# One hybrid attention and SSD layer on one core: gated attention written over its gate, V's tile in places of its own, decays loaded in halves, scores half a chunk sooner, a new order in each head

## The chip, the cores and the metric

The kernel runs on one core of one Trainium2 chip. The metric is the time of one execution on the device in microseconds (us); below 1% this kernel's runs do not tell a change from none. Engines are named as the profile names them: PE (TensorE, matmuls), PEld (its weight loads), DVE (VectorE), ACT (ScalarE), POOL (GpSimd), SP (SyncE). An engine works through its own list in order; it waits where an instruction needs a semaphore that another engine or a DMA has yet to raise.

## The reference, cut to what matters

```python
h = rmsnorm(x, pre_norm_g);  proj = h @ w_in        # 2048 -> q, k, v, z_attn, z_ssm, xBC, dt
o = dilated_attention(q, k, v, rel_bias_table)      # 16 heads x 128, three windows merged
attn_out = rmsnorm(o, attn_norm_g) * silu(z_attn)
ssm_out = ssd_branch(z_ssm, xBC, dt_raw, ...)       # conv, bidirectional chunked scan, D skip, gate, norm
mix = concat([attn_out, ssm_out]) @ w_out
y = x + rmsnorm(mix, post_norm_g)                   # once for 512 prompt rows, once for 256 sample rows
...
# ssd_scan, one direction, chunks of 128 rows:
decay = exp(a_cs[l] - a_cs[s])                      # within a chunk, causal
y_diag = (C B^T * decay) @ xc                       # "within"
y_off = C @ state_before_chunk * exp(a_cs)          # "across"
```

## The kernel before, in words

The 512 prompt rows and the 256 sample rows are held together as T = 768 columns, features on the partitions. Float32 matrices are multiplied in three passes: each operand is split into a rounded part (`_hi`, made by ACT) and the rest (`_lo`, made by DVE), and PE adds hi*hi, hi*lo and lo*hi. Up to about 1271 us of the span PE makes most of the projections and parks them in DRAM (`zx_scr`: V, both gates `za` and `zs`, the SSD's x, half of Q). The stretch that the change touches follows: sixteen turns of `head(a)`, a = 0 to 15, one attention head and two SSD heads each, written out by hand on every engine. From about 1975 us on comes the output projection, which is not touched.

In each `head(a)` PE also works through the rest of the projection (`stream_half`: 12 half chunks a head, for K and half of Q of the heads to come), as filler between the steps of the head. Its steps: `within_chunks(a - 1)` (y_diag of the head before, reads `decay`), `scores(a)` and `scores_of_sample(a)`, `turn_probs(a)` (transposes of the probabilities), `turn_probs_of_sample(a)`, `attend(a)`, `turn_x(a)`, `turn_v(a + 1)` (transposes of x, and of the next head's V), `across_chunks(a)` (y_off). Head a's scores stand in four banks of `ps`, from which DVE takes them (`biased_maxima`, which writes `probs`), ACT makes the exponentials (`exp_of_scores`), and DVE scales them (`normalised`).

Buffers are few, and that makes the waits. `oT`, the attention output, is the front of `probs`: so `biased_maxima(a)` waits until the store of the gated `oT` of head a - 1 has landed in DRAM (`ua_stored`). `decay` (128 x 3072 numbers: two directions, d = 0 and d = 1, of 1536) is loaded from `loc_scr` by one DMA on ACT's queue, `load_decays`, once `within_chunks(a - 1)` has read its d = 0 part, which holds the weights summed over both directions (`weights_in_chunks`, semaphore `wmat_done`). Then DVE subtracts (`decay_differences`, which stands ahead of `normalised` in its list), limits (`decay_limited`), ACT takes the exponential (`exp_of_decays`) and DVE weights (`weighted_decays`). `vT` holds V of the next head; it is loaded by `load_v_and_x` after `attend`. POOL issues the stores of the gated results and the loads of `er`, `cb` (every fourth head) and Q.

The waits that the prediction uses most:

```python
def scores(a):                      # PE
    pe.wait_ge(tile_out, tile_of("k", a) + 1)
    ...
        pe.wait_ge(diag_read, a)    # y_summed(a - 1) on DVE has read what within_chunks(a - 1) left in ps
def turn_probs(a):
    pe.wait_ge(normed, 6 * a + 4)   # normalised(a) on DVE
```

## Time and profile before

| | |
|---|---|
| time, median of 3 runs | 2471.28 us (2469.89 to 2485.74) |
| profiled execution, own time | 2472.09 us |
| its span in the trace | 2470.3 us |
| granted TensorE clock, mean | 0.993 |
| PE busy | 2409.2 us, 98% |
| DVE busy | 1786.7 us, 72% |
| ACT busy | 995.1 us, 40% |

Busy is time in which an engine had at least one instruction under way; PE's instructions overlap, so a busy PE isn't PE at its peak. The span leaves out 1.8 us around the trace. The three runs' median lies 0.8 us below the profiled execution.

### The profile page before, as it was taken

What the parts mean: (1) busy time and instruction counts of PE and PEld (TensorE: products, weight loads), DVE (VectorE), ACT (ScalarE), POOL (GpSimd) and SP (SyncE); (2) the same over time, 40 slices, a digit from 0 to 9 for tenths busy, and PEclk for the clock granted to TensorE, in tenths of its full rate; (3) what the DMA queues carried; (4) which work ended last, traced back from release to release, by engine and by line L of the source; (5) the groups of instructions that cost most, each with busy time, mean ns of one, the idle gap of its engine ahead of it and who ended that gap; (6) DMA issues with size and microseconds to landing.
All of it is one profiled execution on the core that took longest, in us unless ns stands there. A gap on an engine that the chain in (4) does not pass through costs nothing. (4 is left out here: it accounts for less than half of the span.)

```text
span 2470.3 us, 36360 instructions
## 1 busy us (share of the span) xinstructions
PE 2409.2 (98%) x13604; PEld 2280.5 (92%) x13604; DVE 1786.7 (72%) x2563; ACT 995.1 (40%) x1664; POOL 466.1 (19%) x750
## 2 busy tenths in 40 slices
PE   7999999999999999999999999999999999999998
PEld 7999999999999999999998889899889888888887
DVE  5676766666666677777758778777878768777867
ACT  6333433333333333333335455454545532333332
POOL 0000277777773011111100000000000000000000
PEclk9999999999999999999999999999999999999999
DMA  5235466666665344443474555556555435445544
GB/s 167 72 112 182 126 198 206 204 205 200 200 199 158 114 128 132 127 125 119 122 242 145 184 184 160 182 179 193 156 192 167 139 133 170 151 156 130 175 160 164
DMA packets 318345, 398.81 MB, mean 161 GB/s; under 512 B 22822, under 2 KB 238310, under 8 KB 315287
## 3 DMA queue, kind: packets, MB, share of 16 engines
q1 hardware_dynamic: 266103, 225.20, 29.8%
q0 software_dynamic: 29168, 95.62, 12.2%
q10 hardware_dynamic: 22960, 76.53, 9.0%
q8 instruction: 65, 1.06, 0.2%
q14 instruction: 49, 0.40, 0.0%
HBM read 309.02 MB, written 95.59 MB: 164 GB/s over the span
## 5 line engine op out<-in xcount | busy, mean ns | idle before, releaser
L1166 PE MATMUL ps<-h_hi,w_hi 128*128 128x384 f32 x1088 | 365.2, 336 | 0.0
L1166 PE MATMUL ps<-h_lo,w_hi 128*128 128x384 f32 x1088 | 365.0, 335 | 0.0
L1166 PE MATMUL ps<-h_hi,w_lo 128*128 128x384 f32 x1088 | 364.6, 335 | 0.0
L2443 DVE TENSOR_TENSOR w_lo<-raw_qk,w_hi 128x512 fp32r<-128x512 f32 x272 | 214.3, 789 | 154.6 <-ACT w_hi L1696 153.2
L1166 PE MATMUL ps<-t_hi,w_lo 128*128 128x384 f32 x816 | 276.0, 338 | 0.0
L1166 PE MATMUL ps<-t_hi,w_hi 128*128 128x384 f32 x816 | 275.6, 338 | 0.0
L1166 PE MATMUL ps<-t_lo,w_hi 128*128 128x384 f32 x816 | 275.0, 337 | 0.0
L1696 ACT ACTIVATE w_hi<-raw_qk 128x512 fp32r<-128x512 f32 x272 | 171.2, 630 | 244.7 <-PE ps L1166 244.7
L1030 PE MATMUL ps<-h_hi,w_hi 128*128 128x384 f32 x768 | 205.2, 348 | 0.0
L1166 PEld LDWEIGHTS ps<-h_lo,w_hi 128*128 128x128 f32 x1088 | 204.3, 188 | 0.0
L1166 PEld LDWEIGHTS ps<-h_hi,w_lo 128*128 128x128 f32 x1088 | 204.2, 188 | 0.0
L1166 PEld LDWEIGHTS ps<-h_hi,w_hi 128*128 128x128 f32 x1088 | 204.2, 188 | 0.0
L1030 PE MATMUL ps<-h_lo,w_hi 128*128 128x384 f32 x768 | 197.5, 338 | 0.0
L1030 PE MATMUL ps<-h_hi,w_lo 128*128 128x384 f32 x768 | 197.0, 337 | 0.0
L1166 PEld LDWEIGHTS ps<-t_hi,w_lo 128*128 128x128 f32 x816 | 153.3, 188 | 0.0
L1166 PEld LDWEIGHTS ps<-t_hi,w_hi 128*128 128x128 f32 x816 | 153.1, 188 | 0.0
L1166 PEld LDWEIGHTS ps<-t_lo,w_hi 128*128 128x128 f32 x816 | 153.1, 188 | 0.0
L2443 DVE TENSOR_TENSOR w_lo<-stage,w_hi 128x512 fp32r<-128x512 f32 x136 | 99.9, 735 | 71.5 <-ACT w_hi L1696 71.0
L2752 DVE TENSOR_TENSOR stage<-stage,ps 128x512 f32<-128x512 f32 x144 | 97.1, 685 | 71.8 <-PE ps L1328 70.9
L1696 ACT ACTIVATE w_hi<-stage 128x512 fp32r<-128x512 f32 x136 | 85.6, 630 | 151.1 <-PE ps L1166 114.5
L1399 ACT ACTIVATE w_hi<-w_raw 128x512 fp32r<-128x512 f32 x140 | 85.6, 626 | 150.5 <-PE ps L911 88.4
L1328 PE MATMUL ps<-h_hi 128*128 128x512 f32 x372 | 145.2, 390 | 0.0
(370 smaller groups left out, 5411.9 us busy)
## 6 DMA issues: line engine op xcount, KB each, us to landing
raw_qk<-in_w_in SPq DMA_DIRECT2D x102, 512.0 KB, 4.3
w_raw<-in_w_in SPq DMA_DIRECT2D x144, 256.0 KB, 3.5
stage<-loc_scr ACTq DMA_DIRECT2D x16, 1536.0 KB, 11.9
stage<-t_scr SPq DMA_DIRECT2D x48, 512.0 KB, 3.8
stage<-zx_scr ACTq DMA_DIRECT2D x61, 384.0 KB, 5.2
stage<-in_w_out SPq DMA_DIRECT2D x36, 512.0 KB, 3.7
stage<-in_w_in SPq DMA_DIRECT2D x34, 512.0 KB, 4.2
zx_scr<-w_raw SPq DMA_DIRECT2D x34, 384.0 KB, 3.3
```

The lines of the kernel that those rows point to most:

```text
L1030: last = nc.tensor.matmul(ps[:, 2 * parity + b, 0:HALF_T], w, h[:, k * T + b * HALF_T:k * T + (b + 1) * HALF_T], start=(c == 0 and kk == 0 ...
L1166: ins = nc.tensor.matmul(ps[:, bank, 0:HALF_T], w, h(k), start=(start and kk == 0 and q == 0), stop=(last and kk == KC - 1 and q == 2), sk ...
L1328: last = nc.tensor.matmul(ps[:, bank, :], m, w, skip_group_check=True, start=(k == 0 and q == 0 and (p == 0 or not chained)), stop=(k == G ...
L1399: nc.scalar.activation(w_hi[:, c, :], w_raw[:, c, :], ACT.Copy).then_inc(w_hi_done, 1)
L1696: nc.scalar.activation(w_hi[:, n_slot(n, pp), :], src, ACT.Copy).then_inc(w_hi_done, 1)
L2443: nc.vector.tensor_tensor(w_lo[:, n_slot(n, pp), :], src, w_hi[:, n_slot(n, pp), :].bitcast(f32), ALU.subtract).then_inc(w_lo_done, 1)
L2752: ins = nc.vector.tensor_tensor(acc[:, o:o + NBW], acc[:, o:o + NBW], ps[:, bank, :], ALU.subtract if turned else ALU.add)
```

## The change

- `attention_gated` writes `oT * za` into `za` and not into `oT`, and POOL stores `za`. The wait for `ua_stored` leaves `biased_maxima` on DVE and stands on ACT ahead of the load of the next `za`, which moves from `load_head` to `load_behind_scores`.
- V is loaded into two pieces that lie elsewhere (`v_part`, 384 columns each, in `sq_c` and `loc_ssum`), by two DMAs, right after V of the head before has been copied out of `ps`: about a head sooner.
- `load_decays(a, d)`: d = 1 is loaded near the end of the head before, after `wmat_done`; d = 0 as before after `within_chunks`.
- PE: `scores(a)` starts one half chunk sooner, two half chunks instead of one stand between the two turns of probabilities, one instead of two between `attend` and `turn_v`, three instead of two ahead of `across_chunks`.
- New order in each head on ACT and DVE, and in the preparation of head 0, where POOL holds its loads of `er` and `cb` until V has landed.

```diff
+        v_part = (sq_c[:, P:P + HALF_T], loc_ssum[:, TT * 64:TT * 64 + HALF_T])
...
-                pool.dma_start(u_scr[a * P:(a + 1) * P, :], oT).then_inc(ua_stored, 16)
+                pool.dma_start(u_scr[a * P:(a + 1) * P, :], za).then_inc(ua_stored, 16)
...
             load_q(0)
+            pool.wait_ge(v_in, 32)
             load_er(0)
...
             def turn_v(i):
-                pe.wait_ge(v_in, 16 * i + 16)
+                pe.wait_ge(v_in, 32 * i + 32)
...
-                stream_halves(a, 1, 2)
+                stream_halves(a, 1, 1)
                 scores(a)
                 scores_of_sample(a)
-                stream_halves(a, 3, 4)
+                stream_halves(a, 2, 4)
                 turn_probs(a)
-                stream_halves(a, 7, 1)
+                stream_halves(a, 6, 2)
                 turn_probs_of_sample(a)
                 attend(a)
+                stream_halves(a, 8, 1)
                 turn_x(a)
-                stream_halves(a, 8, 2)
                 if a < LAST:
                     turn_v(a + 1)
-                stream_halves(a, 10, 2)
+                stream_halves(a, 9, 3)
                 across_chunks(a)
...
-            def load_decays(a):
-                act.dma_start(decay.rearrange("p (d n) -> p d n", d=2),
-                              loc_scr.rearrange("(d h) t -> d (h t)", d=2)[:, a * 2 * T:(a + 1) * 2 * T]
+            def load_decays(a, d):
+                if a > 0 and d == 1:
+                    act.wait_ge(wmat_done, a)
+                act.dma_start(decay[:, 2 * T * d:2 * T * (d + 1)].rearrange("p (o n) -> p o n", o=1),
+                              loc_scr.rearrange("(d h) t -> d (h t)", d=2)[d:d + 1, a * 2 * T:(a + 1) * 2 * T]
                               .partition_broadcast(P)).then_inc(decay_in, 16)
...
             def load_head(a):
                 act.wait_ge(diag_ready, 2 * a)
-                load_decays(a)
-                if a < LAST:
-                    act.wait_ge(att_gated, a)
-                    load_zx(za, ZX_ZA, a, za_in)
+                load_decays(a, 0)
...
                     if a > 0:
+                        act.wait_ge(ua_stored, 16 * a)
+                        load_zx(za, ZX_ZA, a, za_in)
                         act.wait_ge(y_gated, a)
                         load_zx(zs, ZX_ZS, a, zs_in)
...
-            def load_v_and_x(i):
-                act.wait_ge(pv_ready, 2 * i)
-                load_zx(vT, ZX_V, i, v_in)
-                load_xs(i)
+            def load_v(i):
+                for half in range(2):
+                    act.dma_start(v_part[half], zx_scr[(ZX_V + i) * P:(ZX_V + i + 1) * P,
+                                                       half * HALF_T:(half + 1) * HALF_T]).then_inc(v_in, 16)
...
             load_first_xs()
-            load_zx(vT, ZX_V, 0, v_in)
+            act.wait_ge(xc_out, XC_OUT + 48 * (HEADS - 1))
+            load_v(0)
             load_strip(0)
+            load_decays(0, 0)
+            load_decays(0, 1)
             load_zx(za, ZX_ZA, 0, za_in)
             load_zx(zs, ZX_ZS, 0, zs_in)
-            load_decays(0)
...
             def biased_maxima(a):
                 dve.wait_ge(strip_in, 16 * a + 16)
-                if a > 0:
-                    dve.wait_ge(ua_stored, 16 * a)
...
-                nc.vector.tensor_tensor(oT, oT, za, ALU.mult).then_inc(att_gated, 1)
+                nc.vector.tensor_tensor(za, oT, za, ALU.mult).then_inc(att_gated, 1)
```

DVE from the rest of V (`v_lo`) in head 5 to the first bias and maximum of head 6, before:

```order
L2358 TENSOR_TENSOR v_lo<-ps,v_hi 128x384 [waits vt_out] x2
L2131 TENSOR_TENSOR osq_sum<-osq_sum,stage 128x768 [waits o_sq]
L2270 TENSOR_TENSOR stage<-stage 128x1536 [waits dve_seq]
...
L2378 TENSOR_TENSOR stage<-ps,stage 128x768 [waits off_ready,er_in]
...
L2372 TENSOR_TENSOR stage<-stage 128x768 [waits z_silu,dve_seq,o_sq]
...
L2402 TENSOR_TENSOR stage<-stage,ps 128x768 [waits dve_seq,diag_ready]
L2411 TENSOR_TENSOR stage<-stage 128x768 [waits z_silu,diag_read]
L2294 ISA stage,cur<-ps,stage 128x512 [waits scores_ready,ua_stored,strip_in]
```

The same place on DVE after the change, from the weighting of the decays on:

```order
L2138 TENSOR_TENSOR stage<-stage 128x1536 [waits cb_in,decay_exp]
L2138 TENSOR_TENSOR stage<-stage 128x1536
L2138 TENSOR_TENSOR osq_sum<-osq_sum,stage 128x768 [waits o_sq]
L2277 TENSOR_TENSOR stage<-stage 128x1536 [waits dve_seq]
...
L2363 TENSOR_TENSOR v_lo<-ps,v_hi 128x384 [waits vt_out] x2
...
L2377 TENSOR_TENSOR stage<-stage 128x768 [waits z_silu,dve_seq,o_sq]
L2383 TENSOR_TENSOR stage<-ps,stage 128x768 [waits off_ready,er_in]
...
L2407 TENSOR_TENSOR stage<-stage,ps 128x768 [waits dve_seq,diag_ready]
L2416 TENSOR_TENSOR stage<-stage 128x768 [waits z_silu,diag_read]
L2299 ISA stage,cur<-ps,stage 128x512 [waits scores_ready,strip_in]
```

The sum of squares and `weights_in_chunks` (the row of 128x1536 that waits for `dve_seq`) moved ahead of V's rest, the gated product (`z_silu`, `o_sq`) ahead of `across_read`, and `ua_stored` is gone from the last row.

ACT from the gates of head 5 to the loads that open head 6, before (`loc_scr` holds the decays, `zx_scr` the gate `za`):

```order
L1544 ACTIVATE stage<-stage 128x768 [waits za_in]
L1544 ACTIVATE stage<-stage 128x768 [waits zs_in]
L1399 ACTIVATE w_hi<-w_raw 128x512 [waits tile_done,w_in3]
L1412 ACTIVATE k_hi<-ps 128x768 [waits sscores_ready,tile_done]
L1551 DMA stage<-loc_scr 128x2x1536 [waits diag_ready]
L1560 DMA stage<-zx_scr 128x768 [waits att_gated]
L1595 ACT_TABLE_LOAD
```

ACT at the same place after the change:

```order
L1546 ACTIVATE stage<-stage 128x768 [waits za_in]
L1546 ACTIVATE stage<-stage 128x768 [waits zs_in]
L1555 DMA stage<-loc_scr 128x1536 [waits wmat_done]
L1401 ACTIVATE w_hi<-w_raw 128x512 [waits w_used,w_in2]
L1401 ACTIVATE w_hi<-w_raw 128x512 [waits tile_done,w_in3]
L1414 ACTIVATE k_hi<-ps 128x768 [waits sscores_ready,tile_done]
L1555 DMA stage<-loc_scr 128x1536 [waits diag_ready]
L1596 ACT_TABLE_LOAD
```

One half of the decays is now issued three ACT instructions ahead of the other, and `za` no longer follows them.

In the middle of head 5 ACT stood before as follows, from the rounding of the turned probabilities on:

```order
L1631 ACTIVATE pT_hi<-ps 128x512 [waits pt_ready] x4
L1636 ACTIVATE pTs_hi<-ps 128x512 [waits pts_ready]
L1548 ACTIVATE stage<-stage 128x3072 [waits decay_arg]
L1560 DMA stage<-zx_scr 128x768 [waits pv_ready]
L1560 DMA stage<-zx_scr 128x768 [waits ys_stored,sum_d_out]
```

ACT at the same place after the change:

```order
L1634 ACTIVATE pT_hi<-ps 128x512 [waits pt_ready] x4
L1550 ACTIVATE stage<-stage 128x3072 [waits decay_arg]
L1639 ACTIVATE pTs_hi<-ps 128x512 [waits pts_ready]
L1401 ACTIVATE w_hi<-w_raw 128x512 [waits w_used,w_in0]
L1648 ACTIVATE stage<-ps 128x512 [waits pv_ready]
```

The exponential of the decays (128x3072) moved ahead of the rounding of the sample's probabilities.

## Rows read from the trace of the kernel before

**Rows 1.** The page, part 1: busy time, share of the span, instructions.

```profile
PE 2409.2 (98%) x13604; PEld 2280.5 (92%) x13604; DVE 1786.7 (72%) x2563; ACT 995.1 (40%) x1664; POOL 466.1 (19%) x750
```

**Rows 2.** Waits of PE, 1283 to 1975 us: who waited for whom, total, times, longest.

```profile
PE ps L1068 <- DVE stage L2318: 17.5, 8, 4.2
PE ps L1058 <- DVE cur L2294: 10.0, 7, 1.9
PE ps L1361 <- DVE h_lo L2640: 3.9, 1, 3.9
```

**Rows 3.** Windows, one for each head (4, 14, 15), and the sum of all 16.

```profile
1455.38:1501.81 46.43, 42.25 (x265) 40.18 (x265) 33.85 (x56) 21.63 (x37) 3.43 (x6) 0.96 0.58 195
...
1893.85:1935.09 41.24, 40.77 (x265) 38.69 (x265) 34.44 (x56) 21.31 (x37) 2.88 (x5) 1.00 0.52 155
1935.09:1974.71 39.62, 33.65 (x199) 32.09 (x199) 29.89 (x47) 21.83 (x37) 1.15 (x2) 0.95 0.47 161
sum 691.36, PE 655.31 PEld 619.57 DVE 546.26 ACT 343.66 POOL 41.67; mean PE 40.96 PEld 38.72 DVE 34.14 ACT 21.48 POOL 2.60
```

**Rows 4.** Waits of DVE, 1283 to 1975 us.

```profile
DVE stage L2131 <- DMA stage<-loc_scr: 36.7, 12, 6.2
DVE stage L2294 <- DMA u_scr<-stage: 19.7, 7, 3.3
```

**Rows 5.** Timeline of DVE in head 4: start, length, what, idle before.

```profile
1466.32 3.36 DVE L2131 TENSOR_TENSOR stage<-stage,loc_ssum 128x3072 f32<-128x3072 f32 x1 [6.19 <-DMA stage<-loc_scr]
...
1469.80 1.67 DVE L2318 TENSOR_SCALAR stage<-stage,cur 128x512 f32<-128x512 f32 x4
```

**Rows 6.** Windows in head 4: length, busy PE, PEld, DVE, ACT, POOL, granted clock.

```profile
1467.00:1471.50 4.50, 0.34 (x2) 0.02 (x1) 4.46 (x7) 0.00 (x0) 0.00 (x0) 1.00 0.88 353
...
1473.00:1474.50 1.50, 1.50 (x9) 1.50 (x7) 0.91 (x5) 0.99 (x3) 0.00 (x0) 0.50 0.00 0
```

**Rows 7.** DMA issues, 1283 to 1971 us: count, KB each, median us to landing.

```profile
stage<-loc_scr ACTq DMA_DIRECT2D x15, 1536.0 KB, 11.8
...
stage<-zx_scr ACTq DMA_DIRECT2D x57, 384.0 KB, 5.1
u_scr<-stage POOLq DMA_DIRECT2D x30, 384.0 KB, 8.2
```

**Rows 8.** Timeline of PE in head 5, from the first half chunk behind the scores.

```profile
1507.39 0.34 PE L1030 MATMUL ps<-h_hi,w_hi 128*128 128x384 f32 x1
...
1515.74 1.91 PE L1068 MATMUL ps<-sq_c,stage 128*128 128x128 f32 x16
...
1533.78 3.29 PE L1134 MATMUL ps<-stage 128*128 128x128 f32 x28
```

**Rows 9.** Timeline of DVE in head 5.

```profile
1505.82 0.69 DVE L2294 CUSTOM_DVE_ANT_0 stage<-ps,stage 128x512 f32<-128x512 f32 x1 [3.24 <-DMA u_scr<-stage]
...
1523.53 3.43 DVE L2131 TENSOR_TENSOR stage<-stage 128x1536 f32<-128x1536 f32 x2
1526.88 2.23 DVE L2254 TENSOR_TENSOR stage<-stage,coef 128x256 f32<-128x256 f32 x4
...
1532.97 1.76 DVE L2270 TENSOR_TENSOR stage<-stage 128x1536 f32<-128x1536 f32 x1
...
1542.52 0.94 DVE L2402 TENSOR_TENSOR stage<-stage,ps 128x768 f32<-128x768 f32 x1
```

**Rows 10.** Timeline of ACT in head 5.

```profile
1520.73 2.77 ACT L1548 ACTIVATE stage<-stage 128x3072 f32<-128x3072 f32 x1
...
1533.78 1.58 ACT L1544 ACTIVATE stage<-stage 128x768 f32<-128x768 f32 x2
```

**Rows 11.** Timeline of PE ahead of head 0.

```profile
1274.82 1.54 PE L1117 MATMUL ps<-sq_c,stage 128*128 128x128 f32 x6 [3.63 <-DMA stage<-zx_scr]
```

**Rows 12.** Timeline of DVE ahead of head 0.

```profile
1270.63 0.68 DVE L2083 TENSOR_SCALAR stage<-stage,conv_cols,vec_cols 128x772 f32<-128x772 f32 x1 [8.25 <-DMA stage<-zx_scr]
1271.35 4.20 DVE L2086 SCALAR_TENSOR_TENSOR stage<-stage,conv_cols 128x772 f32<-128x772 f32 x4
```

More of the change, by code:

```diff
@@ L1117, in turn_v @@
                         last = nc.tensor.transpose(ps[:, bank, q * P:(q + 1) * P],
-                                                   vT[:, c * P:(c + 1) * P], ident)
+                                                   v_part[half][:, q * P:(q + 1) * P], ident)
                     last.then_inc(vt_ready, 1)
@@ L1808, in _ @@
             v_rounded(0)
+            load_v(1)
             k_rounded(0)
@@ L1826, in head @@
                 probs_rounded(a)
+                exp_of_decays(a)
                 sample_rounded(a)
[L1828 to L1839 removed]
                 if i % 2:
                     k_rounded(i)
+                stream_hi(m + 2)
+                attended(a)
+                attended_sample(a)
+                squared(a)
+                stream_hi(m + 3)
+                x_turned(a)
+                v_rounded(i)
+                if a > 0:
+                    load_xs(i)
+                if i < LAST:
+                    load_v(i + 1)
+                if i % 2 == 0:
+                    q_rounded(i)
+                silu_of_gates(a)
+                load_decays(i, 1)
                 stream_hi(m + 4)
[L1843 removed]
+                stream_hi(m + 5)
                 if i % 2:
                     q_rounded(i)
[L1846 to L1847 removed]
+                else:
                     k_rounded(i)
@@ L1881, in _ @@
             attended(LAST)
+            act.wait_ge(ua_stored, 16 * LAST)
             tile_ready(tile_of("za", LAST))
@@ L2593, in head @@
                 normalised(a)
+                stream_lo(m)
                 decay_limited()
@@ L2596, in head @@
                 probs_lo(a)
-                if i % 2 == 0 and a < LAST:
-                    q_lo_of(i)
-                stream_lo(m)
+                stream_lo(m + 1)
                 sample_lo(a)
-                stream_lo(m + 1)
-                stream_lo(m + 2)
                 weighted_decays(a)
+                if a < LAST:
+                    square_added(a)
+                weights_in_chunks()
                 scaled_x(a)
                 if a == LAST:
-                    weights_in_chunks()
                     return
                 v_lo_of(i)
-                square_added(a)
-                weights_in_chunks()
+                if i % 2 == 0:
+                    q_lo_of(i)
+                stream_lo(m + 2)
                 stream_lo(m + 3)
@@ L2613, in head @@
                     k_lo_of(i)
-                across_read(a)
                 stream_lo(m + 4)
                 attention_gated(a)
+                across_read(a)
+                stream_lo(m + 5)
                 if i % 2:
                     q_lo_of(i)
-                stream_lo(m + 5)
+                else:
+                    k_lo_of(i)
                 skip_added(a)
-                if i % 2 == 0:
-                    k_lo_of(i)
             for a in range(HEADS):
```

22 lines of the change are left out of this document (2 added, 20 removed).

## The prediction

> **What bounds the kernel now.** Read the busy shares first: PE is busy 98% of the span, DVE 72%, ACT 40% [rows 1]. So time can only be won where PE stands still, or where it runs slowly because it stood still. The waits of PE in the stretch of the sixteen heads show where: 17.5 us in 8 waits ahead of the turn of the probabilities (L1068, for `normalised` on DVE), 10.0 us in 7 waits ahead of the sample's scores (L1058, for the first maximum on DVE), 3.9 us once behind the last head [rows 2]. The windows, head by head, show what a head costs with and without them: 46.43 us in head 4, which has one long wait, 41.24 us in head 14, which has none of the two kinds, 691.36 us for all sixteen up to the first matmul of the output projection [rows 3].
>
> Why does DVE come late? Its own waits answer: 36.7 us in 12 waits for the landing of the decays, 19.7 us in 7 waits for the landing of the gated attention's store [rows 4]. Head 4 shows the first kind: `decay_differences` idles 6.19 us, starts at 1466.32, and behind it stands `normalised`, for which PE waits [rows 5]. During that PE has no work from 1467 to 1471.5, and afterwards it is granted 0.50 of its clock, the 1.2 GHz level, in the window from 1473.0 to 1474.5 [rows 6]; so a 4.2 us wait costs more than 4.2 us. The second kind is the first maximum in head 5, 3.24 us late [rows 9].
>
> **The floor.** I take PE's busy time in a head at full clock, 40.77 us in head 14 [rows 3], as the time of a head without long waits. It overlaps itself at restarts and so holds a few tenths of short waits, which I leave in, since some will stay. Fifteen heads: 691.36 - 39.62 = 651.7 us now, 15 x 40.8 = 612.0 us then: 39.7 us at most for the whole of heads 0 to 14. What follows asks how much of that the change gets.
>
> **Gate and store.** The product goes into `za`, so `probs` is free when its readers on PE and ACT are done. The 19.7 us of DVE's second kind go, and with them PE's 10.0 us ahead of L1058. DVE's instructions are as many as before. The wait moves to ACT, ahead of the load of `za` in `load_behind_scores`; queued behind it are the load of `zs` and the rounding of the turned probabilities, for which DVE and then PE wait. A store takes 8.2 us from issue to landing [rows 7]. The product now stands ahead of `across_read`, some 9 us ahead of the next sample scores, and ACT asks some 6 us after those, so 15 us against 8.2: hidden. Cover gone, each us would cost PE one in every head.
>
> **Decays in halves.** The d = 1 half is issued behind the gates in the head before, at least 6 us ahead of the point at which the whole was; it is covered. The d = 0 half is still issued at `diag_ready`. Its landing isn't in the trace. Bounds: 384 KB from ACT's queue take 5.1 us, 1536 KB take 11.8 us [rows 7]. On the line between them 768 KB take 7.3 us, which I use; the ends are 5.1 and 11.8. Let S be the end of the sample's scores on PE. `diag_ready` comes one half chunk and the scores ahead of S, about 5.7 us, so the half lands at S + 1.6. The turn of the probabilities is due four half chunks behind S, 1515.74 - 1507.39 = 8.35 us [rows 8]. DVE needs 3.36 for the differences, 0.2 for the reciprocal and 1.67 for `normalised` [rows 5]: 5.2 us, start by S + 3.1. So it holds, with 1.5 us to spare, and the 17.5 us go, with the slow clock behind four or five of them. In heads 4, 8 and 12 `cb` is loaded as well, and the landing may come a few us later: up to 1 us of wait in each is in my residue.
>
> The Trainium skill, DMA: Bandwidth & Descriptors (Anatomy of one DMA; Measured), gives about 2.0 us plus bytes over 436 GB/s and advises batches of 1 MiB and more. By that the whole would land in 5.6 us, the half in 3.8 us, and the decays would never have been waited for; the trace does not agree, with 11.8 us [rows 7], and the measurement decides. Its advice speaks against both splits; it would bring a second fixed part to V, which has a whole head of time now, so the sum stays as it is by either.
>
> **V in its own places.** Its load is a head early, one DMA more on ACT's queue. PE's wait for V inside the heads is small and no longer there. The remaining wait of `turn_v` is for ACT's two copies of the attention output (`o_out`). It is now one half chunk plus x's transposes behind `attend`, 2.7 us, less than before. ACT's copies take about 1.0 us and start 0.4 us behind PE: 1.3 us to spare.
>
> **The order within a head**, counted from S. The second turn of probabilities is two half chunks behind the first: 8.35 + 1.7 + 4.2 = S + 14.2. ACT's exponential of the decays, 2.77 us [rows 10], now ahead of the sample's rounding, starts at S + 11.1 (behind ACT's four copies of the turned probabilities, estimated at 2.7 us from the turn's start) and ends at S + 13.9: just in time. DVE: sample's rest by S + 16.2, `weighted_decays` 3.43, the sum of squares 1.0 (ACT's square is done at S + 20.0), `weights_in_chunks` 1.76, `scaled_x` 2.23, V's rest 1.0 [rows 9] gives S + 26.0. `across_chunks` waits for these two; in head 5 it came at 1533.78 - 1507.39 = 26.4 behind S [rows 8], and now there is one half chunk more between (ten instead of nine): S + 28. Two us to spare.
>
> Then DVE is tight. `across_read` can start at S + 30.9, when most of `across_chunks` (3.29 us, [rows 8]) is done. Behind it stand 1.3 us of its own, 0.6 for a chunk's rest, 0.9 for K's or Q's, 1.7 for `skip_added`: S + 35.4, and `y_summed`, 0.94 us [rows 9], ends at S + 36.4. PE has `across_chunks` to S + 31, a half chunk and `within_chunks` to S + 34.7, and now only one half chunk to the scores, which wait for `y_summed`: due at S + 36.8. Before there were two. 0.4 us to spare, from ACT's side less: the gates' SiLU (1.58 us, [rows 10], and a table load) now stands ahead of two chunks' rounding, which end near S + 30. I take 0.0 to 1.0 us a head for this and keep 40.8 as the head's time, which holds some 0.5 us of it.
>
> **Last head and first.** Head 15 takes 39.62 us to the first matmul of the projection, with 2.1 us of wait, 5% of its clock missing, and 3.9 us of wait behind it [rows 2, 3]. It gets one half chunk more behind its scores (2.1 us), loses the first wait and the slow clock, and keeps part of the last, since DVE's list behind `weighted_decays` is what PE waits for and starts 1 us sooner with the exponential ahead: about 37.5 us against 41.7, so -4 us (bounds -2 and -6). Ahead of head 0 PE waits 3.63 us for V [rows 11], but the first chunk behind is not ready before the convolution on DVE (4.20 us from 1271.35) and the rest behind it [rows 12]. x and V are now alone in the queues with Q and the strip, so DVE's 8.25 us wait for x [rows 12] shortens by 2 to 3 us: -2.5 us (bounds 0 and -4).
>
> **Sum.** 39.7 + 4 + 2.5 = 46 us. Profiled execution 2472.1 - 46 = 2426 us; the median of the runs shown lies 0.8 us lower, so 2425 us. The projection behind the heads and everything ahead keep their time.
>
> **Rivals.**
> - *DVE becomes the bound at the head's end.* It is busy 34 of 41 us a head [rows 3], without a gap from S + 15.5 to the maxima by the sum above. If `y_summed` ends 1 to 2 us late, the scores wait in every head: 16 x 0.8 to 16 x 1.8, 2438 to 2454 us. For it: 0.4 us of slack in a chain of fifteen steps. Against it: each step's time is known. Chance 0.16.
> - *The half of the decays lands hardly sooner than the whole*, since other queues fill the engines at that time (the load of `er`, two stores). At 10 to 11.8 us it is S + 4.3 to S + 6.1, PE waits 1.2 to 3.0 us a head: 2444 to 2472 us. For it: a DMA of four times the bytes takes only 2.3 times as long [rows 7], so bytes alone don't set it. Chance 0.08, of which half ends within 1% of the time before.
> - *The change doesn't do what it says:* a wait of the same length takes the place of the one removed, as `ua_stored` on ACT or the clock's slow phases from other short waits. 2450 to 2475 us, chance 0.05.
> - *Slower than before:* the exponential of the decays now blocks ACT ahead of the sample's rounding. Landing, then 3.36 + 0.2 + 1.67 + 0.7 + 1.8 on DVE, 2.77 + 0.6 on ACT, 0.7 on DVE: 11.8 us to the sample's second product, due at S + 17.4. It is hit from a landing at S + 5.6 on, and a head is slower than the 43.4 us of now from about S + 8.5, a half that takes 14.2 us, longer than the median of the whole. At 16 us a head would take 45.2 us and the kernel 2500 us. Chance 0.02.
> - The forecast has the rest, 0.69, with 2416 to 2437 us of its own.
>
> **Range and chances.** The low end is all short waits gone too (0.5 us a head, 8 us, and the outer bounds): 2414. The high end takes in most of the first rival: 2450. This kernel's measurement tells 1%, 25 us, from no change, so faster means under 2446.6 us: 0.69 + 0.13 + 0.03 + 0.01 = 0.86; slower 0.02; same 0.12.
>
> **What the profile of the changed kernel would show.** Right: no wait of DVE for `loc_scr` over 1 us outside heads 4, 8, 12; no wait for `u_scr` on DVE; PE's windows of 40.3 to 41.5 us a head at a granted clock of 1.00; half decays with 7 to 8 us to landing; across and scores without waits over 1 us. Wrong: waits of PE at the scores for `y_summed` over 1 us in every head (first rival); waits at the turn of probabilities with the decays behind them (second); waits at `turn_v` for ACT's copies, which would say that ACT's list is later than I count it.

## The result, and the profile of the changed kernel

The changed kernel is not faster; if anything it is slower. Its median is 2496.7 us (2495.1 to 2501.7, 4 runs) against 2471.3 us (4 runs) for the kernel before, 25 us more. The ratio of the means is 1.0092, with a 95% interval of 1.0058 to 1.0126: clear of 1, but still within the 1% below which this kernel's runs do not tell a change from none. I had forecast 2425 us, and 72 us lie between. The profiled execution took 2501.65 us, with a span of 2499.8 us.

First the waits of PE in the changed kernel, 1283 to 2010 us (who waited for whom, total, times, longest):

```profile
PE ps L1070 <- DVE stage L2323: 50.3, 13, 7.5
PE ps L1052 <- DVE v_lo L2363: 4.4, 1, 4.4
PE ps L1052 <- DVE stage L2407: 4.0, 8, 0.8
PE ps L1363 <- DVE h_lo L2645: 0.8, 1, 0.8
```

Against [rows 2]: the 10.0 us at the sample's scores are gone and the last wait is down from 3.9 to 0.8 us, as forecast. But the wait ahead of the turn of the probabilities (L1070 now), which I had expected to vanish, went from 17.5 us in 8 to 50.3 us in 13. The scores wait for `y_summed` (L2407) 0.8 us at most.

Next the windows: head 4, head 10, head 14, the stretch from head 15 to the first matmul of the output projection, and all sixteen together.

```profile
1461.20:1512.70 51.50, 43.51 (x267) 41.39 (x265) 34.09 (x57) 21.95 (x37) 3.43 (x6) 0.90 0.54 175
1742.60:1789.50 46.90, 42.22 (x265) 40.10 (x264) 33.88 (x57) 21.85 (x37) 2.90 (x5) 0.96 0.51 156
1929.90:1970.80 40.90, 40.46 (x265) 38.60 (x265) 33.94 (x57) 21.64 (x37) 2.90 (x5) 1.00 0.49 152
1970.80:2005.60 34.80, 33.99 (x210) 32.72 (x210) 30.64 (x48) 21.29 (x36) 1.14 (x2) 1.00 0.45 158
1284.50:2005.60 721.10, 666.04 (x4170) 635.17 (x4170) 547.02 (x887) 349.24 (x593) 41.81 (x72) 0.96 0.52 163
```

The stage of the heads takes 721.1 us, 29.7 more than the 691.36 of before [rows 3]; that is the whole difference of the spans (29.5). Head 14, which waits for nothing, takes 40.90 us, within 0.1 of the 40.8 that I gave each head. Head 4 takes 51.50: its wait, and a granted clock of 0.90 of full speed. Heads 0 to 14 together take 686.3 us, 74 more than the 612.0 that I forecast; 50 of these are the waits at the turn, and the rest is almost all PE's own work at the slower clock that follows such waits (it is busy for 632.0 us there, 606.9 in experiment 12).

DVE says what it is late for. Its wait, and its timeline in head 4 (start, length, what, idle before):

```profile
DVE stage L2138 <- DMA stage<-loc_scr: 77.3, 14, 9.5
```

```profile
1475.51 3.36 DVE L2138 TENSOR_TENSOR stage<-stage,loc_ssum 128x3072 f32<-128x3072 f32 x1 [9.54 <-DMA stage<-loc_scr]
```

Against [rows 4, 5] the wait for the decays has doubled, 36.7 to 77.3 us, and 6.19 us in head 4 became 9.54. The other row of [rows 4], DVE's wait for the store, has gone. ScalarE waits for DMAs too, for the weights that SyncE loads:

```profile
ACT w_hi L1401 <- DMA w_raw<-in_w_in: 46.3, 13, 7.6
```

The DMA issues of the changed kernel, 1283 to 1990 us (count, KB each, median us to landing):

```profile
stage<-loc_scr ACTq DMA_DIRECT2D x30, 768.0 KB, 14.4
w_raw<-in_w_in SPq DMA_DIRECT2D x89, 256.0 KB, 11.0
...
stage<-zx_scr ACTq DMA_DIRECT2D x42, 384.0 KB, 4.6
```

Half of the bytes takes longer to land than the whole did: 14.4 us against 11.8 [rows 7]. Head by head, from the issue and landing times in the trace: in heads 1 to 13 the first half takes 13.9 to 18.3 us and the second 10.3 to 16.3. In heads 14 and 15 they take 5.5 and 7.7, and 5.2 and 7.1 us.

The first half's figure is too kind. Both halves count up one semaphore, and where both are in flight, the counts that are read as the first half's are partly the second's. The packets tell more. Each half is 128 packets of 6144 B. In each of heads 1 to 13 exactly 112 of the first half's start within 7 us of its issue, and the next one not before 9.7 us; the 16 that are missing are one eighth, the share of 2 engines out of 16. Counted in order, the first half is complete only 17.6 to 19.2 us after its issue. In heads 14 and 15 all 128 start within 4.3 us. What is different in the last two? ScalarE's queue around v_rounded in head 3, where head 4's halves are issued:

```profile
1446.17 0.59 ACTq L1527 DMA_DIRECT2D strip_scr<-brow_scr  x1
1446.31 0.51 ACT L1671 ACTIVATE v_hi<-ps 128x384 fp32r<-128x384 f32 x1
1446.80 0.57 ACTq L1527 DMA_DIRECT2D strip_scr<-brow_scr  x1
1447.46 0.38 ACTq L1564 DMA_DIRECT2D stage<-zx_scr  x1
1447.88 0.52 ACTq L1643 DMA_DIRECT2D sq_c<-zx_scr  x1
1448.43 0.45 ACTq L1643 DMA_DIRECT2D loc_ssum<-zx_scr  x1
...
1449.10 0.43 ACTq L1555 DMA_DIRECT2D stage<-loc_scr  x1
...
1459.14 0.33 ACTq L1555 DMA_DIRECT2D stage<-loc_scr  x1
```

`v_rounded(i)` ends with two calls of `make_strips`, which copy part of the position bias strips of later heads from one DRAM buffer to another, and only `if i + 2 < HEADS`: heads 14 and 15 have no such copies ahead of their decays. Here x, both pieces of V and the first half stand within 3 us behind them. In the kernel before, the next thing on this queue came 10 us later:

```profile
1486.77 0.59 ACTq L1525 DMA_DIRECT2D strip_scr<-brow_scr  x1
1487.40 0.57 ACTq L1525 DMA_DIRECT2D strip_scr<-brow_scr  x1
1497.66 0.38 ACTq L1551 DMA_DIRECT2D stage<-loc_scr  x1
```

What the copies do on the DMA engines I counted from the packets in the trace of the changed kernel: how many engines' worth of packets is under way in each us, for the copies (3584 B packets on ScalarE's queue) and for all queues.

```
us      copies   all
1450      2.1   15.2
1453      2.0   14.0
1456      1.8   15.7
1473      0.0    2.0
1474      0.0    2.0
```

The copies keep 2 engines of 16 busy for about 11 us (1447 to 1458). And at the end of the second half (it lands at 1475.5) only two engines are still working: the other 14 are done by 1473. Of the 256 packets of both halves 224 have started by 1464.4; the last 32, two engines' share, start one after the other from 1465.3 to 1474.4.

**Theory 1:** the copies, on 2 DMA engines, hold back everything issued behind them on ScalarE's queue; the change moved V's pieces and the first half right behind them. **Theory 2:** two DMAs cost more than one, by a fixed part each. **Theory 3:** the middle of a head is crowded (stores, weights, `er`, x), whatever ScalarE's queue holds. **Theory 4:** the new order within a head is too tight. A further candidate, SyncE's late weights (11.0 us, the row above), is not on this path in head 4, where DVE starts at 1475.51 and the second half has landed at 1475.48; experiment 9 comes back to it.

### The profile page after: what moved, and what is told of

It is laid out like the page before. It is cut to its first block and busy times, and to the rows that moved or that the text cites. A ratio compares the mean times of both kernels' runs of the same rounds, so it can differ in the third digit from the quotient of the medians.

```text
span 2499.8 us, 36393 instructions
## 1 busy us (share of the span) xinstructions
PE 2415.7 (97%) x13604; PEld 2291.9 (92%) x13604; DVE 1788.6 (72%) x2563; ACT 1000.9 (40%) x1664; POOL 465.2 (19%) x750
## 5 line engine op out<-in xcount | busy, mean ns | idle before, releaser
L2448 DVE TENSOR_TENSOR w_lo<-raw_qk,w_hi 128x512 fp32r<-128x512 f32 x272 | 209.0, 769 | 153.4 <-ACT w_hi L1699 152.3
L2448 DVE TENSOR_TENSOR w_lo<-stage,w_hi 128x512 fp32r<-128x512 f32 x136 | 104.7, 771 | 77.5 <-ACT w_hi L1699 77.3
```

The lines of the kernel that those rows point to most:

```text
L2448: nc.vector.tensor_tensor(w_lo[:, n_slot(n, pp), :], src, w_hi[:, n_slot(n, pp), :].bitcast(f32), ALU.subtract).then_inc(w_lo_done, 1)
```

## Experiments

Each kernel is timed against the kernel before on the same chip; the ratios carry their 95% intervals. The first four ran together, as did the next four and the last four; the kernel before had medians of 2478.5, 2475.8 and 2474.7 us there. Ratios can be compared from one group to the next, a few us cannot.

**1. The changed kernel, strips at the beginning.** All sixteen heads' strips in four DMAs; the calls in `v_rounded` go.

```diff
-                act.dma_start(strip_scr[h * P:(h + 2) * P, :].rearrange("(h p) t -> h p t", h=2)[:, part * n:(part + 1) * n, :],
-                              bass.AP(brow_scr.tensor, h * BROW + P - 1 - part * n, [[BROW, 2], [-1, n], [1, STRIP]])
+                act.dma_start(strip_scr[:, :].rearrange("(h p) t -> h p t", h=HEADS)[:, part * n:(part + 1) * n, :],
+                              bass.AP(brow_scr.tensor, P - 1 - part * n, [[BROW, HEADS], [-1, n], [1, STRIP]])
...
-                act.wait_ge(strip_out, 64 * (i // 2) + 64)
+                act.wait_ge(strip_out, 64)
...
-                if i + 2 < HEADS:
-                    for part in range(2):
-                        make_strips(i // 2 * 2 + 2, 2 * (i % 2) + part)
```

> The changed kernel, with the decay strips of all sixteen heads copied once, at the program's beginning, in four DMAs whose outer dimension is the 16 heads; in the heads none is issued. Theory 1 (the two strip copies of a head, which keep 2 of the 16 DMA engines busy for some 10 us, hold back V's pieces and the decay halves that are issued right behind them on ScalarE's queue): the halves of heads 0 to 13 land as those of heads 14 and 15 do now, in 5 to 8 us instead of 10 to 18; VectorE's wait for the decays falls from 77.3 us in 14 to under 10, PE's wait for the differences from 50.3 us to under 10, and the stage of attention from 720 us to 675 to 685; the kernel takes 2435 to 2460 us, the beginning a few us longer. Theory 2 (two halves cost more than one whole, by a fixed part of each DMA): the landings stay at 10 us and more, the kernel at 2485 to 2500. Theory 3 (the time of the head's middle is crowded by stores, weights and x, whatever ScalarE's queue holds): landings fall by less than a third, the kernel to 2475 to 2490. Theory 4 (the new order within a head is too tight): the decays land early, and PE waits for VectorE's v_rounded or for y_summed instead, 2470 us or more.

Measured: 2430.2 us, ratio 0.9803 (0.9775 to 0.9831). Its PE waits from 1283 us on, DVE's wait for the decays and their landing:

```profile
PE ps L1052 <- DVE stage L2404: 3.6, 8, 0.5
PE ps L1070 <- DVE stage L2320: 1.5, 3, 0.7
...
DVE stage L2135 <- DMA stage<-loc_scr: 16.5, 11, 2.7
```

```profile
stage<-loc_scr ACTq DMA_DIRECT2D x30, 768.0 KB, 6.6
w_raw<-in_w_in SPq DMA_DIRECT2D x87, 256.0 KB, 3.6
```

14.4 us became 6.6, 50.3 us of PE's wait became 1.5, and the time is 5 us below the range that I expected. The change itself is a gain of 2%, and the copies took it and 0.9% more. Theory 2 and theory 4 fall: the halves are still two DMAs, and the order within a head is the same.

**2. The kernel before, the same edit.**

> The kernel before, with the same edit: all strips at the beginning, none in the heads. Theory 1: in the kernel before, the strip copies are over when the decays are issued some 11 us later, so that the whole's landing stays near 11.8 us and the time within 0.5% of the kernel before, 2460 to 2475 us; what the edit gives the changed kernel it doesn't give this one. Theory 3 (everything on the DMA engines is crowded, strips among the crowd): this one gains as much as the changed kernel does, 20 us or more.

Measured: 2481.8 us, ratio 1.0002 (0.9980 to 1.0025). Its waits of PE and DVE and two landings:

```profile
PE ps L1068 <- DVE stage L2315: 27.0, 13, 4.4
...
DVE stage L2128 <- DMA stage<-loc_scr: 54.6, 15, 6.4
```

```profile
stage<-loc_scr ACTq DMA_DIRECT2D x15, 1536.0 KB, 12.7
...
u_scr<-stage POOLq DMA_DIRECT2D x32, 384.0 KB, 4.7
```

The ratio is as theory 1 has it (the time is above my 2460 to 2475 us because the kernel before took 2478.5 us here). The whole lands no sooner without the copies (12.7 us against 11.8), so theory 3 falls as an account of the halves. The edit was not idle, though. The row of the stores, 4.7 us against 8.2 [rows 7], mixes two kinds, and the attention's own say it better: in the kernel before seven of them took 6.8 to 8.1 us, and here none takes over 5.3. The wait at the sample's scores is gone. But then the wait for the whole, which comes next, is longer (27.0 us against 17.5). One wait took the place of the other, and heads 0 to 14 take 651.6 us as before.

**3. The changed kernel, copies behind the first half** (a function `strips_of(i)` holds the three lines, and `head` calls it behind `load_decays(i, 1)`).

```diff
                 load_decays(i, 1)
+                strips_of(i)
```

> The changed kernel, with each head's two strip copies issued behind the first half of the decays instead of ahead of V's pieces and of it. Theory 1: the first half lands in some 6 to 9 us; the strips have then until the second half, some 10 us on; the second half lands as it does now or sooner, since less is piled up: the kernel takes 2440 to 2475 us. Theory 2: no change, 2490 to 2505. Theory 3: no change beyond 5 us.

Measured: 2462.9 us, ratio 0.9941 (0.9913 to 0.9969). Now the first half lands in 5.8 to 7.2 us in heads 1 to 14, and the second, behind the copies, in 9.8 to 12.6 (heads 1 to 13); PE's wait at the turn is 27.1 us in 13. Moving the copies past one DMA freed that one and left the next. (The first half has landed before the second is issued here, so that each landing is its own.)

**4. The kernel before, copies ahead of its decays** (`strips_of(a)` as the first line of `load_head`).

```diff
             def load_head(a):
+                strips_of(a)
                 act.wait_ge(diag_ready, 2 * a)
                 load_decays(a)
```

> The kernel before, with each head's two strip copies issued just ahead of its decays (one DMA of 1536 KB) instead of 11 us sooner. Theory 1: the decays, whose share of the two engines stands behind the copies, land in 18 to 22 us instead of 11.8, so that some 6 to 10 us are lost in each of 14 heads: 2530 to 2600 us, or at least 2500. Theory 2 and 3, by which the copies' place on the queue matters little: within 0.5% of the kernel before, 2465 to 2480 us.

Measured: 2537.4 us, ratio 1.0232 (1.0198 to 1.0266). The theory's direction and the size of the time are right; the landing is not:

```profile
PE ps L1068 <- DVE stage L2322: 70.2, 13, 9.3
...
DVE stage L2135 <- DMA stage<-loc_scr: 92.4, 15, 10.5
```

```profile
stage<-loc_scr ACTq DMA_DIRECT2D x15, 1536.0 KB, 15.3
```

15.3 us in the median (14.7 to 20.4 in heads 1 to 13), not 18 to 22. The edit explains it: the copies stand ahead of the wait for `diag_ready` and so go out 6.0 us before the decays, not just ahead of them. From 10.3 us before to 6.0 us is all that they were moved, and the last of the copies' packets start 8.6 to 11.1 us behind the issue of the decays (0.1 to 0.8 us in the kernel before): they are issued later, and with more traffic of other queues beside them they take 14 to 16 us instead of 10. This one kernel makes the old order suffer from the same copies: their place on the queue is the cause, not the change's other parts.

**5. Strips at the beginning, V's second load behind `k_rounded(0)`.** In the changed kernel PE waited 4.4 us for `v_lo` ahead of head 0, and ScalarE's queue was held for 7.04 us by the issue of V's first piece:

```profile
1272.81 0.59 ACTq L1527 DMA_DIRECT2D strip_scr<-brow_scr  x1
1273.44 7.04 ACTq L1643 DMA_DIRECT2D sq_c<-zx_scr  x1
```

```diff
             v_rounded(0)
-            load_v(1)
             k_rounded(0)
+            load_v(1)
```

> The changed kernel with all strips at the beginning, and in the preparation of head 0 the load of the next head's V behind k_rounded(0) instead of ahead of it. If the 4.4 us that PE waited ahead of head 0 came from ScalarE's queue being held by that DMA's issue, the first head starts some 5 us sooner than in the run with strips first alone (1287.8 us there), and the kernel takes 2423 to 2427 us, my prediction for the change; if it came from something else, 2429 to 2431.

Measured: 2429.5 us, ratio 0.9812 (0.9796 to 0.9828); the first head starts at 1286.9 us against 1287.8. My premise was wrong: the long issue came only where copies had gone out shortly before. In experiment 1 that wait is not there to be won, and in experiment 9, whose preparation still issues the first two copies ahead of V, it stands at 5.1 us.

**6. Extra copies on 16 engines, in the old place.** A `spread_copy` in `v_rounded` copies 4 rows of 16 heads into rows that nobody reads; strips are at the beginning.

```diff
+            def spread_copy(j):
+                row = HEADS * P + 64 * j
+                act.dma_start(strip_scr[row:row + 64, :].rearrange("(h p) t -> h p t", h=HEADS),
+                              bass.AP(brow_scr.tensor, P - 1 - 4 * j, [[BROW, HEADS], [-1, 4], [1, STRIP]])
+                              ).then_inc(spread_out, 16)
```

> The changed kernel with all strips at the beginning, and at the place in each head where the changed kernel issues its two strip copies, two copies of the same source, rows, packets and bytes (4 rows of each of 16 heads instead of 32 rows of each of 2), whose outer dimension is 16; nobody reads them, they are extra work. Theory 1 in its narrow form (it is that the copies lie on 2 engines): they take 2 us rather than 10, the decay halves land in 6 to 9 us, and the kernel stays within 10 us of 2430. Theory 3 (it is their bytes and packets, wherever they lie): the kernel goes back to 2480 to 2500 us.

Measured: 2431.2 us, ratio 0.9819 (0.9800 to 0.9839).

```profile
stage<-loc_scr ACTq DMA_DIRECT2D x30, 768.0 KB, 7.6
...
strip_scr<-brow_scr ACTq DMA_DIRECT2D x26, 224.0 KB, 2.9
```

The same bytes in the same place cost nothing that can be measured: 2.9 us each, and the halves behind them land in 7.6. What hurt is that the copies lie on two engines.

**7. Strips at the beginning, both halves at the head's start.**

```diff
                 load_decays(a, 0)
+                load_decays(a, 1)
...
                 silu_of_gates(a)
-                load_decays(i, 1)
```

> The changed kernel with all strips at the beginning, but both halves of the decays issued at the head's start, where the kernel before issued the whole: the early half is undone, everything else of the change stays. My prediction's term for the halves was 17.5 us, and here the differences are due a little sooner than before, as the rest of the change shortens the head's start: with the pair landing in 12 to 13 us as the whole did, PE waits 3 to 5 us for the differences in each of 15 heads, 2480 to 2500 us. If instead the rest of the change brings the gain (V, gate and order) and the halves little, 2435 to 2450.

Measured: 2469.5 us, ratio 0.9971 (0.9959 to 0.9982), 10 us below the range that I expected, and 20 us above that of the other account.

```profile
PE ps L1070 <- DVE stage L2320: 30.3, 15, 3.4
```

PE's wait is 2 us in each head, not 3 to 5; DVE waits 60.4 us in 15 for the decays, and heads 1 to 14 take 41.5 to 45.5 us. Both halves have landed 9.2 to 12.8 us (median 11.2) after the first is issued, no later than the whole in experiment 2 (12.7 us): two DMAs cost no more than one here. Of the 1.97% that experiment 1 gains, the early half brings 1.68%, 41 us; what the rest of the change saves is, without it, waited out at the decays.

**8. The kernel before with strips at the beginning and halves only.** `load_decays(i, 1)` stands behind `silu_of_gates(a)`, everything else is as before.

> The kernel before with all strips at the beginning (which by itself changed nothing: ratio 1.0002) and the decays in halves, the first of them issued behind the gates' SiLU as in the changed kernel; V, gate and order as before. By my prediction's terms the halves alone give 17.5 us plus what the earlier end of the differences gives VectorE, and the 10 us at the sample's scores stay: 2450 to 2465 us. If the halves only pay with the new order (in the old one something else is late at once, such as y_summed or the attention's store): within 0.4% of 2478.

Measured: 2441.1 us, ratio 0.9849 (0.9829 to 0.9868), faster than I expected by 9 us.

```profile
PE ps L1117 <- DMA stage<-zx_scr: 8.2, 6, 5.9
PE ps L1361 <- DVE h_lo L2641: 3.6, 1, 3.6
PE ps L1030 <- DVE w_lo L2041: 1.1, 1, 1.1
```

The 10.0 us at the sample's scores, which I had booked to the gate, are gone without it: the attention's store lands in 3.4 us (median) once the copies are out of its way. So halves alone give 1.5%, and V, gate and order 0.3% alone; together they give 2.0%. Where the rest comes from is seen when the span is split: heads 0 to 14 take 614.0 us here against 611.9 in experiment 1, so within the heads the halves do nearly everything. The first head starts at 1297.2 us against 1287.8, with 5.9 us of the wait in the first row ahead of it. The rest of the change pays there.

**9. The changed kernel, copies on SyncE's queue at the same moment.**

```diff
+                if r == 0 and 1 <= i and i + 2 < HEADS:
+                    sp.wait_ge(vt_out, 2 * i + 2)
+                    for part in range(2):
+                        h, q, n = i // 2 * 2 + 2, 2 * (i % 2) + part, P // 4
+                        sp.dma_start(strip_scr[h * P:(h + 2) * P, :].rearrange("(h p) t -> h p t", h=2)[:, q * n:(q + 1) * n, :],
...
                 load_w(chunk_at(m), STREAM_COLS[j], c)
```

> The changed kernel with the two strip copies of a head issued by SyncE, on its DMA queue, at the same moment (once v_rounded is done) instead of by ScalarE; everything else as changed, two outer rows and so two DMA engines as well. If what is behind the copies on their own queue is all that suffers, ScalarE's decay halves land in 6 to 9 us, SyncE's weights late instead: 2435 to 2460 us. If the two engines are the bound whichever queue feeds them, the halves land in 9 us and more: 2460 to 2500 us. As the packets of two queues take turns on an engine, I expect the halves between, 8 to 10 us, and 2450 us.

Measured: 2427.6 us, ratio 0.9805 (0.9789 to 0.9821), better than I expected.

```profile
stage<-loc_scr ACTq DMA_DIRECT2D x30, 768.0 KB, 8.3
w_raw<-in_w_in SPq DMA_DIRECT2D x87, 256.0 KB, 14.1
...
strip_scr<-brow_scr SPq DMA_DIRECT2D x26, 224.0 KB
```

Two engines, the same moment, another queue: the halves land in 8.3 us, and now SyncE's weights are late (14.1 us against 3.6 in experiment 1). They have room: ScalarE waits 9.3 us for them in all, and no wait of PE stems from that. So weights that land this late, and later than the changed kernel's 11.0 us, do not by themselves make the kernel slow. This is the sharpest of the runs: for the decays it is the place behind the copies in their own queue that hurts. But other queues are not free of the copies. The first half, which is issued right behind them in time, takes 8.8 us (median of heads 1 to 13) against 6.2 in experiment 1. And in the changed kernel, where the copies are on ScalarE's queue, SyncE's weights took 11.0 us against 3.6. A likely reason, argued and not shown: a load of weights has 32 packets of 512 B on each engine and a half of the decays 8 of 6144 B, so that with turns between the queues the weights wait out more of the copies' packets (0.16 us each).

**10. The kernel before with halves only, copies where they were.**

> The kernel before with the decays in halves and nothing else changed: the strip copies stay in the heads, where the kernel before has them (with strips at the beginning the halves gave 1.5%). The first half is issued some 4 us behind the copies here. Theory 1: its share of the two engines stands behind them, as in the changed kernel, and lands in 10 us and more, but there is room until it is needed; the second half, at the head's start, is free of them: 2445 to 2470 us. If the halves gain nothing as long as the copies are there, within 0.4% of the kernel before.

Measured: 2450.3 us, ratio 0.9905 (0.9890 to 0.9920). The halves land in 9.2 us (median); counted by packets, as the semaphore is shared here too, the first of them takes 10.7 to 14.3 us in heads 1 to 13, as theory 1 has it. PE's wait at the turn is gone, and the waits for the store remain:

```profile
PE ps L1058 <- DVE cur L2298: 10.9, 13, 1.6
DVE stage L2298 <- DMA u_scr<-stage: 33.7, 12, 3.7
```

So with the copies in place the halves win 1% in the old order, where the first of them is issued 4.3 us behind the second copy (1480.93 to 1485.27 us in one head) and nothing else stands between; in the changed kernel it is 2.3 us, with x and V's pieces between, and all of the gain and more is lost.

**11. The changed kernel, copies behind the loads that follow the scores.**

```diff
                 load_behind_scores(a)
+                strips_of(i)
                 probs_rounded(a)
```

> The changed kernel with each head's two strip copies moved from behind v_rounded to behind the loads that follow the scores, some 18 us away from V's pieces and the first half on one side and 12 us behind the second half on the other, still on 2 engines and ScalarE's queue. Theory 1: both halves and the V pieces are clear of them, and the kernel stands where it stands with all strips at the beginning, without that one's wait of 3.6 us near the program's start: 2422 to 2435 us. If a copy on two engines costs wherever it is (20 us in each 41 us are taken on them), 2450 us and more.

Measured: 2424.2 us, ratio 0.9803 (0.9788 to 0.9818). The copies are as many, on as few engines, on the same queue; with 15 us to the next DMA behind them they cost nothing. (The halves land in 6.8 us.)

**12. The best version: strips at the beginning, behind the first group of the B and C projection**, with experiment 5's later load of V.

```diff
-            for part in range(4):
-                make_strips(0, part)
             bc_steps(0, None)
+            for part in range(4):
+                make_strips(0, part)
```

> The changed kernel with all strips copied at once, V's second load behind k_rounded(0), and the four copies behind the first group of the B and C projection instead of ahead of it. In the run with them ahead of it PE waits 3.6 us for the step sizes (softplus on VectorE, whose bias rows come by a DMA), which neither kernel of the comparison did, and the first head starts at 1286.9 us instead of 1281.7. If it is the copies that hold these rows up, this gives 4 to 5 us: 2422 to 2426 us. If not, 2428 to 2431.

Measured: 2422.8 us, ratio 0.9787 (0.9774 to 0.9800), the fastest of all. The wait that the strips had caused near the start, in experiment 1

```profile
PE ps L989 <- DVE stage L2165: 3.9, 1, 3.9
```

is not in this kernel's trace, and its first head starts at 1281.5 us. Its windows, heads 0 to 14 and then head 15 to the first matmul of the output projection:

```profile
1281.50:1893.70 612.20, 606.85 (x3962) 580.50 (x3961) 515.33 (x840) 325.19 (x555) 40.77 (x70) 1.00 0.57 176
1893.70:1928.50 34.80, 34.00 (x210) 32.71 (x210) 30.73 (x48) 21.29 (x36) 1.15 (x2) 1.00 0.45 155
```

## Why the prediction was wrong

*The step that failed* is in "Decays in halves": the d = 1 half "is issued behind the gates in the head before, at least 6 us ahead of the point at which the whole was; it is covered". I looked at when it is issued and not at what stands ahead of it on the queue. The change took ScalarE's loads from a place 10 us behind the strip copies to one right behind them, and no part of my working names these copies, though they are in `v_rounded`, the line above. In the changed kernel the first half is complete 17.6 to 19.2 us after its issue, the second, pushed back in turn, after 10.3 to 16.3. With that a term of the sum fails: the second half's landing, for which I used 7.3 us and gave 11.8 as the worst. Experiments 3, 4, 9 and 11 move the copies alone, and the time follows; experiment 6 keeps their bytes and spreads them, and it does not.

*The rivals.* "The half lands hardly sooner than the whole" is what came, with the sign that I named for it (waits at the turn of probabilities with the decays behind them), but with a wrong cause (other queues) and a bound that was too kind: I took the landing of the whole as the worst case of the half. Its arithmetic holds beyond the bound. A half of 12.7 us, the median of the second halves, lands at S + 7.0, and PE waits 3.9 us in each of 13 heads, 51 us; 50.3 were measured. The slower rival names a half of over 14.2 us and 2500 us, and 2497 us came. That is a coincidence: its mechanism, ScalarE's exponential ahead of the sample's rounding, would make PE wait at the sample's probabilities, and no such wait is in the trace. I gave it 0.02. I never asked what could make a half late. The Trainium skill, DMA: Bandwidth & Descriptors (Why a DMA increments its semaphore by 16 and not by 1), says that a DMA is split over the largest number of engines up to 16 that divides the slowest dimension of both of its patterns: two for these copies. The traces agree (2.0 engines and 10 us for two copies, against 2.9 us for each with an outer 16). Had I applied this to each DMA that the moved ones now follow, I would have seen it. The section Anatomy of one DMA, which the prediction cites from the same page of the Trainium skill, gives its 2.0 us plus bytes over 436 GB/s for DMAs that GpSimd issues; the decays are on ScalarE's queue, so their 11.8 us are no test of it.

*The rest of the working, with the copies out of the way* (experiment 12, and 11, which moves the copies alone). In us, from the first matmul of each head's scores in the traces:

| kernel | first head starts | heads 0 to 14 | head 15 |
|---|---|---|---|
| before | 1283.4 | 651.7 | 39.6 |
| changed | 1284.5 | 686.3 | 34.8 |
| 7, strips first, halves late | 1290.9 | 647.6 | 36.8 |
| 8, halves only, strips first | 1297.2 | 614.0 | 35.7 |
| 11, changed, copies behind the scores | 1279.8 | 612.0 | 34.8 |
| 12, changed, strips behind the first group | 1281.5 | 612.2 | 34.8 |

- The floor: I forecast 612.0 us for heads 0 to 14; 612.2 measured, at a granted clock of 1.00.
- The half's landing: 7.3 us on the line between two sizes; 6.6 us is the median of all halves, and the one that the sum speaks of, the second, took 6.4 to 10.2 us, median 7.6.
- Gate and store: DVE's wait for the store is gone, in the changed kernel as well. But part of what I booked to it was the copies' doing: experiments 2 and 8 lose the 10 us with the old gate.
- The end of a head: "0.0 to 1.0 us a head" for `y_summed`; 0.5 us at the longest, 3.6 us in 8 (0.8 at the longest in the changed kernel). The first rival did not come.
- Halves against the rest: I gave 17.5 us to the halves; alone they give 37 us (experiment 8), and undoing the early half in the whole costs 41 us (experiment 7). The term was too small, since a wait at the turn took the place of any other that went, and a stretch of slower clock came with it (0.96 and 0.90 of full speed in the long heads above, 1.00 in head 14). That the sum comes out all the same is no merit of this term: it rests on the floor, which takes all waits as gone, whoever caused them.
- Last head: 37.5 us forecast, 34.8 measured.
- First head: 4.6 us sooner forecast (2.5 us of waits, and the half chunk of 2.1 us that moved behind the scores of head 15). It starts at 1283.35 us before (1974.71 less 691.36, [rows 3]), 3.5 us sooner in experiment 11 and 1.8 in experiment 12. In the changed kernel it starts 1.2 us later instead, after 4.4 us of wait. That is the second step to fail. DVE's wait for x did fall, from 8.25 us to 5.8, as I forecast; but "x and V are now alone in the queues" leaves out the load of head 1's V, which is new there and stands behind two copies. Its issue held ScalarE for 7.04 us, and with it `k_rounded(0)`, for which the scores wait. In experiment 11 an issue is held for 7.03 us as well, but behind `k_rounded(0)`, and the 4.4 us are gone.

2425 us was a fair estimate of this change without the copies behind which it put its loads: 2424.2 us in experiment 11, 2422.8 in 12. In part this is luck: the last head came 2.7 us under its term and the first head 1 to 3 over, and the errors cancel.

What stays open: why the issue of a load was held for 7 us ahead of head 0 and for 1.7 us at most in the heads, and how much the copies cost another queue on the same engines. No run varies the size of the packets.

## What to carry to other kernels

When a load is moved, list what stands ahead of it on its new place in the queue, and the number of DMA engines that each of these uses. The copies here, with an outer dimension of 2, are a 10 us plug for their queue, and they are harmless to it where nothing urgent follows for that long (10.3 us in the kernel before, 15 in experiment 11). Take a plug apart by an outer dimension of 16, by distance, or by a queue whose loads have room. And a natural control in the trace (here head 14, without copies ahead of its decays, at 40.9 us) is worth looking for before any experiment.

## What the runs showed of the hardware

- A queue keeps its order on each DMA engine: behind two copies on 2 engines 112 of a 768 KB load's 128 packets start within 7 us and the last 16 much later. The loads took 14.4 us (median), on a free queue 6.6. With the copies in another queue at the same moment they took 8.3, and that queue's 256 KB weights 14.1 instead of 3.6. Other queues feel the copies as well: 11.0 us instead of 3.6 for the weights in the changed kernel. The Trainium skill, DMA: Bandwidth & Descriptors (Queues, rings and completion order), has an engine take turns between its queues a packet at a time; experiment 9 agrees.
- Issuing can stall as well: ahead of head 0 the instruction for a 192 KB load took 7.04 us on ScalarE's queue right behind two such copies. In the heads of the same kernel, also behind two copies but with the load of x between, it took 0.4 to 0.6 us.
- Copying 448 KB in two DMAs, 128 rows of 3584 B, takes 10 us on two engines; each of two copies of 224 KB takes 2.9 us on sixteen.
- The load of 1536 KB lands no sooner when the copies are gone (12.7 us). Two halves issued at one point are both there after 11.2 us (median, experiment 7).
- Where two DMAs in flight raise one semaphore, the landing that the profile gives for the first can be too early: 13.9 to 18.3 us by the semaphore, 17.6 to 19.2 us by the packets.
